# Up projection of a two-block layer: weights stationary, both halves of x as moving columns

## The chip, the cores and the metric

One core of one Trainium2 chip runs the whole program in one launch. The metric is device time in microseconds (us); lower is better.

## The reference, cut to what matters

Two layers run one after the other on x, 256 positions by 1024 features, all in float32. The change touches the MLP of the first:

```python
h2 = rms_norm(x, norm_mlp_g)
x = x + jnp.square(jax.nn.relu(h2 @ w_mlp_up)) @ w_mlp_down     # w_mlp_up 1024x4096, w_mlp_down 4096x1024
```

`rms_norm` scales each position by a positive factor r, so relu(r·a)² = r²·relu(a)², and r² may be applied after the down projection.

## The kernel before

**Products of three.** TensorE multiplies in fp32r, so each operand is split into a high part (rounded to fp32r) and a low part (the rest), and a product is high·high, high·low and low·high, summed in PSUM. Line 477 is the first, 478 multiplies by the low weights, 479 by the low activations.

**Blocks and chunks.** All weight matrices are cut into blocks of 512 columns, in program order, and each block into chunks of 4 tiles of 128 rows (`CK`). Up has 8 blocks of 2 chunks (`B_UP` to `B_UP + 7`), down 2 blocks of 8 chunks (`B_DN`, `B_DN + 1`). Four slots hold chunks. SyncE loads a chunk into `raw` (L391) once `mm_done` says that the chunk four earlier has been used; ScalarE (ACT) writes the high part `w_hi` (L1019, semaphore `split_hi`); VectorE (DVE) writes the low part `w_lo` (L1482, `split_lo`); TensorE (PE) waits for that at the first product of each chunk. `begin(b)` on ACT and DVE issues the splits of the two chunks of block b + 1 (and chunks 2 and up of block b itself, for the down blocks). Each engine does its list in order, and that order is written by hand.

**Before the change**, the activations are stationary: `mm` (L447) loads 128 columns of `s_hi` or `s_lo` and streams 512 weight columns into bank `G[b % 2][t]`, t being one of two tiles of 128 positions. That is 8 tiles x 2 x 3 = 48 products a block. DVE's `relu` (L1900) multiplies by r, takes max(0) and writes `hid`, positions on the partitions; ACT squares it (L1280); PE turns it with 8 transposes (`hidden`, L825) into the banks `M`; ACT rounds it to `hT_hi` (L1286), DVE subtracts to get `hT_lo` (L1906). Down (`mm` with `stat=(hT_hi, hT_lo)`) takes these as stationary. PE's order is block b, then the transposes of block b − 1; those of block 7 come after the first two quarters of `B_DN` (L840). `residual` (L1507) adds a down block to x. PE waits at block b for the release of block b − 2's banks (`ev0`, `ev1`). The rest of DVE's order in a middle block: two splits of the next block, relu of this one, `hidden_lo` of the last.

Of the kernel before, what the change touches and what calls it, by code (L numbers as in the profile page):

```python
# [5 lines left out]
F32 = mybir.dt.float32  # L6
# [5 lines left out]
P = 128  # L12
# [93 lines left out]
def build(nc, x_in, norm_mix_g, w_in, conv_w, a_log, dt_bias, gdn_norm_g, q_norm_g, k_norm_g, w_out,  # L106
# [4 lines left out]
    with ctx:  # L111
        def sb(name, shape, dt=F32, stack=None):
            return (stack or ctx).enter_context(nc.sbuf_tensor(name, shape, dt))
# [3 lines left out]
        def sem(name):  # L117
            if name not in named:
                named[name] = ctx.enter_context(nc.semaphore(name))
            return named[name]  # L120
# [153 lines left out]
        def st(at, n):  # L274
            return sm[:, at:at + n]
# [19 lines left out]
        SSX, RNX = st(28, 8), st(48, 16)  # L295
        XSC = st(68, 8)
        MU, VAR, RSTD = GA_, BT, EG
        RS5H, RS5Q = st(624, 2), st(626, 2)


        P2R = view(ar2, 0, NT, 2048)
# [40 lines left out]
        def at(base, step, i):  # L342
            return base if i is None else base + step * i
# [100 lines left out]
        def _(pe):  # L444
            act_w = (s_hi, s_lo)

            def mm(b, i=None, stat=act_w, turned=None, hidden=None, quarters=None):  # L447


                blk = blocks[b]  # L450
                pairs = range(blk["kt"] // 2) if quarters is None else quarters
                if b >= 2 and pairs[0] == 0:

                    pe.wait_ge(sem("ev0"), at(b - 1, 2, i))
                    pe.wait_ge(sem("ev1"), at(b - 1, 2, i))
                for pair in pairs:
                    c = 2 * pair // CK
                    n = blk["chunk0"] + c
                    kn, width = chunk_shape(b, c)
                    if b == 0:  # L460
                        pe.wait_ge(sem("split_lo" if pair % 2 else "first_lo"), c + 1)
                    elif 2 * pair == CK * c:

                        pe.wait_ge(sem("split_lo_pool" if pool_chunk(b, c) else "split_lo"), at(low_parts(b, c), 4, i))
                    if turned is not None:

                        pe.wait_ge(sem("turn_lo"), turned - KT // 2 + pair + 1)
                    if hidden is not None:

                        pe.wait_ge(sem(hidden), pair + 1)  # L470
                    early = b in EARLY and 2 * pair == blk["kt"] - 2
                    tiles = [(kt, t) for kt in (2 * pair, 2 * pair + 1) for t in range(NT)]
                    for kt, t in sorted(tiles, key=lambda tile: tile[1]) if early else tiles:
                        o = G[b % 2][t][:, 0:width]
                        hi, lo = (s[:, kt, P * t:P * t + P] for s in stat)
                        wh, wl = (s[:, n % SLOTS, kt - CK * c, 0:width] for s in (w_hi, w_lo))
                        nc.tensor.matmul(o, hi, wh, start=kt == 0, stop=False)  # L477
                        nc.tensor.matmul(o, hi, wl, start=False, stop=False)  # L478
                        last = nc.tensor.matmul(o, lo, wh, start=False, stop=kt == blk["kt"] - 1)  # L479
                        if early and t == 0 and kt == blk["kt"] - 1:  # L480
                            last.then_inc(sem("first_tile"), 1)
                    if kt == CK * c + kn - 1:
                        last.then_inc(sem("mm_done"), 1)
# [327 lines left out]

            turn(xtile, lambda q: [("ev0", B_O + 1 + q // 2), ("ev1", B_O + 1 + q // 2), ("turn_lo", 8)])

            def hidden(b, i=None):

                pe.wait_ge(sem("hid_sq"), at(b + 1, 2, i))
                for q in range(2):
                    bank = M[2 * (b % 2) + q]
                    if b >= 2 or i is not None:

                        pe.wait_ge(sem("hid_lo"), at(2 * (b - 2) + q + 1, 4, i))
                    for kk in range(2):
                        for t in range(NT):
                            c = P * (2 * q + kk)
                            last = nc.tensor.transpose(bank[:, (2 * kk + t) * P:(2 * kk + t + 1) * P], hid[:, b % 2, t, c:c + P], ident)  # L825
                    last.then_inc(sem("hid_pe"), 1)

            mm(B_UP, turned=12)
            mm(B_UP + 1)
            hidden(0)  # L830
            mm(B_UP + 2)
            hidden(1)
            with pe.Fori(0, 2) as i:
                for j in range(2):
                    mm(B_UP + 3 + j, i)
                    hidden(2 + j, i)
            mm(B_UP + 7)
            hidden(6)
            mm(B_DN, stat=(hT_hi, hT_lo), hidden="hid_lo", quarters=[0, 1])
            hidden(7)  # L840
            mm(B_DN, stat=(hT_hi, hT_lo), hidden="hid_lo", quarters=range(2, DFF // P // 2))
            mm(B_DN + 1, stat=(hT_hi, hT_lo))


            turn(xtile, lambda q: [("ev0", B_DN + 1 + q // 2), ("ev1", B_DN + 1 + q // 2), ("hid_lo", 16)])
            for j in range(4):
                mm(B_2 + j, turned=None if j else 16)

# [152 lines left out]
        def _(act):  # L1001
# [272 lines left out]
            act.wait_ge(sem("ev1"), B_UP)  # L1274
            squares(1, x)

            def square_hidden(b, i=None):
                for t in range(NT):
                    act.wait_ge(sem(f"ev{t}"), at(B_UP + b + 1, 2, i))
                    ins = nc.scalar.activation(hid[:, b % 2, t], hid[:, b % 2, t], ACT.Square)  # L1280
                ins.then_inc(sem("hid_sq"), 1)

            def hidden_hi(b, i=None):
                for q in range(2):
                    act.wait_ge(sem("hid_pe"), at(2 * b + q + 1, 4, i))
                    nc.scalar.activation(hT_hi[:, bass.ds(at(4 * b + 2 * q, 8, i), 2), :], M[2 * (b % 2) + q].rearrange("p (a b) -> p a b", a=2), ACT.Copy)\  # L1286
                        .then_inc(sem("hid_hi"), 1)

            begin(B_UP)
            square_hidden(0)  # L1290
            with act.Fori(0, 3) as i:
                for j in range(2):
                    begin(B_UP + 1 + j, i)
                    hidden_hi(j, i)
                    square_hidden(1 + j, i)
            begin(B_UP + 7)
            hidden_hi(6)
            square_hidden(7)
            hidden_hi(7)
            begin(B_DN)  # L1300
            begin(B_DN + 1)
# [159 lines left out]
        def _(dve):  # L1461
# [30 lines left out]
            def mm_finished(b, i=None):  # L1492
                dve.wait_ge(sem("mm_done"), at(blocks[b]["chunk0"] + blocks[b]["chunks"], 4, i))
# [397 lines left out]
            mean_squares(1)  # L1891
            dve.wait_ge(sem("root"), root("mlp"))

            def relu(b, i=None):
                mm_finished(B_UP + b, i)
                for t in range(NT):
                    if i is not None or b >= 2:

                        dve.wait_ge(sem("hid_pe"), at(2 * (b - 2) + 2, 4, i))
                    V.tensor_scalar(hid[:, b % 2, t], G[(B_UP + b) % 2][t][:, :], RS[:, 2 + t:3 + t], 0.0, ALU.mult, ALU.max).then_inc(sem(f"ev{t}"), 1)  # L1900

            def hidden_lo(b, i=None):
                for q in range(2):
                    dve.wait_ge(sem("hid_hi"), at(2 * b + q + 1, 4, i))
                    kk = bass.ds(at(4 * b + 2 * q, 8, i), 2)
                    V.tensor_tensor(hT_lo[:, kk, :], M[2 * (b % 2) + q].rearrange("p (a b) -> p a b", a=2), hT_hi[:, kk, :].bitcast(F32), ALU.subtract)\  # L1906
                        .then_inc(sem("hid_lo"), 1)

            begin(B_UP)
            relu(0)  # L1910
            begin(B_UP + 1)
            relu(1)
            hidden_lo(0)
            begin(B_UP + 2)
            relu(2)
            hidden_lo(1)
            with dve.Fori(0, 2) as i:
                for j in range(2):
                    begin(B_UP + 3 + j, i)
                    relu(3 + j, i)  # L1920
                    hidden_lo(2 + j, i)
            begin(B_UP + 7)
            relu(7)
            hidden_lo(6)
            hidden_lo(7)
# [365 lines left out]
```

## Time and profile before

| | us |
|---|---|
| median of 3 runs (950.75, 950.84, 953.18) | 950.84 |
| the profiled execution's own time | 952.35 |
| its span in the profile | 950.5 |
| PE busy in the span | 921.4 |
| mean granted TensorE clock | 0.993 |

Spans and starts are microseconds from the span's start. The up blocks run from about 323 to 416 us, the down blocks from there to 507 us. A matmul's row gives its start and a modelled duration that overlaps the next one's, so the pace is read from start to start.

### The profile page before, as it was taken

The page shows a single profiled execution, that of the slowest core. Times are in us where ns is not written, and L with a number is a line of the kernel's source. Part 1 is how long each engine was busy: PE and PEld are TensorE (multiplying, and loading weights), DVE is VectorE, ACT ScalarE, POOL GpSimd, SP SyncE. Part 2 cuts the span into 40 slices and gives each one's busy share as a digit, 9 for nine tenths or more (in the row PEclk, how much of TensorE's full clock was granted, in tenths as well). Part 3 has the DMA queues.
Part 4 walks back from the last instruction along what each step waited for, and adds up shares of the span by engine and source line. Part 5 has one row for each costly group of instructions (what it writes and reads, how often), then busy time and mean ns, then how long its engine had stood idle before and what let it go on. Part 6 is the DMA issues. An engine that isn't in the chain of part 4 may idle for free.

```text
span 950.5 us, 11857 instructions
## 1 busy us (share of the span) xinstructions
PE 921.4 (97%) x4691; PEld 771.8 (81%) x4691; DVE 591.9 (62%) x816; ACT 451.3 (47%) x654; POOL 124.7 (13%) x82
## 2 busy tenths in 40 slices
PE   8999999998998999999999999999998999999998
PEld 5887788876996888888887889888887888888886
DVE  4469978979456656654445745877774655555542
ACT  5265355963344544453335434753553455454531
POOL 0322112676601000000000002100000000000100
PEclk9999999999998999999999999999999999999999
DMA  7774542432312555555567645343541556554561
GB/s 268 191 247 137 177 133 89 143 124 70 95 45 85 164 193 178 177 177 177 179 192 276 208 143 174 138 133 120 181 144 44 165 164 196 183 177 133 200 221 67
DMA packets 83138, 149.87 MB, mean 158 GB/s; under 512 B 8320, under 2 KB 16048, under 8 KB 82960
## 3 DMA queue, kind: packets, MB, share of 16 engines
q1 hardware_dynamic: 79424, 144.52, 46.9%
q10 hardware_dynamic: 3040, 3.79, 1.1%
q0 software_dynamic: 624, 0.87, 0.8%
q8 instruction: 35, 0.57, 0.2%
q14 instruction: 15, 0.12, 0.0%
HBM read 147.72 MB, written 1.44 MB: 157 GB/s over the span
## 4 chain that ended last, share of the span: by engine, by line
PE 84%; DVE 7%; ACT 4%; DMA 3%; issue 1%; POOL 0%; SPq 0%; DVEq 0%; ACTq 0%
PE gemm L477 23%; PE gemm L479 23%; PE gemm L478 23%; PE mixbank L720 2%; DMA raw<-in_w_in_dram 2%; PE mixbank L612 2%; PE mixbank L587 2%; DVE w_lo L1482 1%; PE mixbank L493 1%; ACT w_hi L1019 1%; ACT junk L1175 1%; PE mixbank L825 1%; PE mixbank L598 1%; DVE mix L1599 1%; ACT mix L1187 1%
## 5 line engine op out<-in xcount | busy, mean ns | idle before, releaser
L1482 DVE TENSOR_TENSOR w_lo<-raw,w_hi 128x2048 fp32r<-128x2048 f32 (+3 forms) x131 | 287.6, 2209 | 177.5 <-ACT w_hi L1019 177.4
L477 PE MATMUL gemm<-w_hi,s_hi 128*128 128x512 f32 (+3 forms) x912 | 354.6, 389 | 11.8 <-DVE w_lo L1482 7.6
L479 PE MATMUL gemm<-w_hi,s_lo 128*128 128x512 f32 (+3 forms) x912 | 347.3, 381 | 0.0
L478 PE MATMUL gemm<-w_lo,s_hi 128*128 128x512 f32 (+3 forms) x912 | 347.1, 381 | 0.0
L1019 ACT ACTIVATE w_hi<-raw 128x2048 fp32r<-128x2048 f32 (+3 forms) x140 | 255.4, 1836 | 167.7 <-DMA raw<-in_w_in_dram 47.6
L477 PEld LDWEIGHTS gemm<-w_hi,s_hi 128*128 128x128 f32 x912 | 172.4, 189 | 46.5 <-issue 10.6
L479 PEld LDWEIGHTS gemm<-w_hi,s_lo 128*128 128x128 f32 x912 | 172.3, 189 | 32.9
L478 PEld LDWEIGHTS gemm<-w_lo,s_hi 128*128 128x128 f32 x912 | 172.6, 189 | 31.0 <-issue 0.5
L2165 POOL TENSOR_TENSOR sm<-sm 128x2 f32<-128x2 f32 (+4 forms) x14 | 29.1, 2077 | 514.4 <-DVE sm L1526 318.8
L2159 POOL TENSOR_TENSOR w_lo<-raw,w_hi 128x2048 fp32r<-128x2048 f32 x9 | 41.4, 4616 | 202.4 <-ACT w_hi L1019 202.4
L477 PE MATMUL gemm<-w_hi,hT_hi 128*128 128x512 f32 x128 | 50.6, 396 | 0.0
L478 PE MATMUL gemm<-w_lo,hT_hi 128*128 128x512 f32 x128 | 50.5, 394 | 0.0
L479 PE MATMUL gemm<-w_hi,hT_lo 128*128 128x512 f32 x128 | 50.4, 394 | 0.0
L1036 ACT ACTIVATE mix<-gemm,sm 128x512 f32<-128x512 f32 (+2 forms) x25 | 16.3, 652 | 67.8 <-PE gemm L479 67.8
L477 PE MATMUL gemm<-w_hi,h_hi 128*128 128x512 f32 x88 | 35.0, 397 | 0.2 <-DVE w_lo L1482 0.2
L479 PE MATMUL gemm<-w_hi,h_lo 128*128 128x512 f32 x88 | 34.8, 395 | 0.0
L478 PE MATMUL gemm<-w_lo,h_hi 128*128 128x512 f32 x88 | 34.8, 395 | 0.0
L1735 DVE SCALAR_TENSOR_TENSOR mix<-mixbank,cw,mix 128x255 f32<-128x255 f32 (+2 forms) x72 | 31.4, 477 | 5.4 <-ACT mix L1187 4.5
L1046 ACT ACTIVATE s_hi<-mixbank,gains 128x256 fp32r<-128x256 f32 x48 | 18.5, 488 | 21.6 <-PE mixbank L493 21.6
L477 PEld LDWEIGHTS gemm<-w_hi,hT_hi 128*128 128x128 f32 x128 | 24.0, 187 | 5.9
L479 PEld LDWEIGHTS gemm<-w_hi,hT_lo 128*128 128x128 f32 x128 | 23.9, 187 | 5.9
L478 PEld LDWEIGHTS gemm<-w_lo,hT_hi 128*128 128x128 f32 x128 | 24.0, 187 | 5.8
(300 smaller groups left out, 950.8 us busy)
## 6 DMA issues: line engine op xcount, KB each, us to landing
raw<-in_w_in_dram SPq DMA_DIRECT2D x40, 1024.0 KB, 5.1
raw<-in_w_mlp_up_dram SPq DMA_DIRECT2D x16, 1024.0 KB, 5.6
raw<-in_w_mlp_down_dram SPq DMA_DIRECT2D x16, 1024.0 KB, 5.1
raw<-in_w_gate_dram SPq DMA_DIRECT2D x10, 1024.0 KB, 5.1
raw<-in_w_up_dram SPq DMA_DIRECT2D x10, 1024.0 KB, 5.2
raw<-in_w_down_dram SPq DMA_DIRECT2D x10, 1024.0 KB, 5.2
raw<-in_w_out_dram SPq DMA_DIRECT2D x8, 1024.0 KB, 5.1
raw<-in_w_xkv_dram SPq DMA_DIRECT2D x8, 1024.0 KB, 5.2
```

What stands on the lines that cost most here:

```text
L477: nc.tensor.matmul(o, hi, wh, start=kt == 0, stop=False)
L478: nc.tensor.matmul(o, hi, wl, start=False, stop=False)
L479: last = nc.tensor.matmul(o, lo, wh, start=False, stop=kt == blk["kt"] - 1)
L587: last = nc.tensor.matmul(M[g % 2][:, j * ns:(j + 1) * ns], qq[:, P * t:P * t + P], kk[:, 0:ns], start=e == 0, stop=e == len(parts) - 1)
L612: last = nc.tensor.matmul(M[3][:, j * width:(j + 1) * width], exps_turned[:, g % 2, (j * per + s) * P:][:, 0:P], values(h, s), start=s == ...
L720: last = nc.tensor.matmul(o, lhsT[:, 4 * u + q, :], blocks_of(rhs[:, 4 * u + q, :], lv, odd), start=True, stop=True)
L1019: nc.scalar.activation(w_hi[:, n % SLOTS, 0:kn, 0:width], raw[:, n % SLOTS, 0:kn, 0:width], ACT.Copy)\
L1046: ins = nc.scalar.activation(s_hi[:, 2 * q + kk, :], M[q][:, SEQ * kk:SEQ * kk + SEQ], ACT.Copy, scale=gains[:, norm, 2 * q + kk:2 * q + k ...
L1482: V.tensor_tensor(w_lo[:, s, 0:kn, 0:width], raw[:, s, 0:kn, 0:width], w_hi[:, s, 0:kn, 0:width].bitcast(F32), ALU.subtract)\
L1735: ins = V.scalar_tensor_tensor(y, M[e % 3][:, SEQ * j:SEQ * j + SEQ - tap], cw[:, 3 - tap, ct:ct + 1], y, ALU.mult, ALU.add)
L2159: pool.tensor_tensor(w_lo[:, s, 0:kn, 0:width], raw[:, s, 0:kn, 0:width], w_hi[:, s, 0:kn, 0:width].bitcast(F32), ALU.subtract)\
L2165: pool.tensor_tensor(dst, src, MHALF[:, 0:n], ALU.pow).then_inc(sem("root"), 1)
```

## The change

The eight up blocks get their own function `up` with the weights stationary; `hid` holds turned values (features on the partitions), so the transposes go; the factor r leaves the up blocks, and the down residual multiplies by r².

```diff
-        s_hi = sb("s_hi", [P, KT, SEQ], F32R)
-        s_lo = sb("s_lo", [P, KT, SEQ], F32R)
+        s_both = sb("s_both", [P, KT, 2, SEQ], F32R)
+        s_hi, s_lo = s_both[:, :, 0, :], s_both[:, :, 1, :]
+        UP_BANKS = [[G[0][0], G[0][1], G[1][0], G[1][1]], M]
-        hid = sb("hid", [P, 2, NT, NCOL], F32, a2)
+        hid = sb("hid", [P, 8, SEQ], F32, a2)
...
 # TensorE: hidden() and the mm() calls of the up blocks go; instead
+            def up(b, i=None):
...
+                def tile_products(kt, f):
+                    n = blocks[B_UP + b]["chunk0"] + kt // CK
+                    o = UP_BANKS[b % 2][f]
+                    wh, wl = (w[:, n % SLOTS, kt % CK, P * f:P * f + P] for w in (w_hi, w_lo))
+                    nc.tensor.matmul(o[:, :], wh, s_both[:, kt].rearrange("p a b -> p (a b)"), start=kt == 0, stop=False)
+                    return nc.tensor.matmul(o[:, 0:SEQ], wl, s_hi[:, kt, :], start=False, stop=kt == KT - 1)
+                pe.wait_ge(sem("split_lo"), at(low_parts(B_UP + b, 0), 4, i))
+                for kt in range(CK):
...
+                    for f in range(4):
+                        last = tile_products(kt, f)
+                last.then_inc(sem("mm_done"), 1)
+                pe.wait_ge(sem("split_lo"), at(low_parts(B_UP + b, 1), 4, i))
...
+                for f in range(4):
+                    for kt in range(CK, KT):
+                        last = tile_products(kt, f)
+                    if f < 3:
+                        last.then_inc(sem("up_pe"), 1)
+                last.then_inc(sem("mm_done"), 1)
...
+            mm(B_DN, stat=(hT_hi, hT_lo), hidden="hid_lo")
 # ScalarE: square_hidden() goes
             def hidden_hi(b, i=None):
+                for f in range(4):
+                    act.wait_ge(sem("hid_sq"), at(4 * b + f + 1, 8, i))
+                    nc.scalar.activation(hT_hi[:, bass.ds(at(4 * b + f, 8, i), 1), :], hid[:, 4 * (b % 2) + f:4 * (b % 2) + f + 1, :], ACT.Copy)\
...
             begin(B_UP)
+            hidden_hi(0)
             with act.Fori(0, 3) as i:
                 for j in range(2):
                     begin(B_UP + 1 + j, i)
+                    hidden_hi(1 + j, i)
             begin(B_UP + 7)
             hidden_hi(7)
 # VectorE: relu() and hidden_lo() go
+            def hidden_low(b, f, i=None):
+                dve.wait_ge(sem("hid_hi"), at(4 * b + f + 1, 8, i))
...
+                V.tensor_tensor(hT_lo[:, kt, :], hid[:, n:n + 1, :], hT_hi[:, kt, :].bitcast(F32), ALU.subtract).then_inc(sem("hid_lo"), 1)
+            def relu_squares(b, i=None):
+                for f in range(4):
+                    if f < 3:
+                        dve.wait_ge(sem("up_pe"), at(3 * b + f + 1, 6, i))
+                    else:
+                        mm_finished(B_UP + b, i)
+                    o, h = UP_BANKS[b % 2][f], hid[:, 4 * (b % 2) + f, :]
+                    V.tensor_copy(h, o[:, SEQ:2 * SEQ]).then_inc(sem("up_half"), 1)
+                    dve.wait_ge(sem("up_half"), at(4 * b + f + 1, 8, i))
+                    ins = V.tensor_tensor(h, o[:, 0:SEQ], h, ALU.add)
...  # ins signals up_sum or ev0/ev1, and DVE waits for that signal
+                    V.scalar_tensor_tensor(h, h, 0.0, h, ALU.max, ALU.mult).then_inc(sem("hid_sq"), 1)
+                    if f >= 1:
+                        hidden_low(b, f - 1, i)
             begin(B_UP)
+            relu_squares(0)
+            hidden_low(0, 3)
...  # a loop over blocks 1 to 7: begin(b), relu_squares(b), hidden_low(b, 3)
+            V.tensor_tensor(RS1Q, RS[:, 2:4], RS[:, 2:4], ALU.mult).then_inc(sem("rs1"), 1)
...  # the down residual
-                residual(B_DN + j, j)
+                    V.scalar_tensor_tensor(cols, G[(B_DN + j) % 2][t][:, :], RS1Q[:, t:t + 1], cols, ALU.mult, ALU.add).then_inc(sem(f"ev{t}"), 1)
```

## Rows read from the trace of the kernel before

**Rows 1.** The page: busy time per engine, granted clock in 40 slices, chain by engine.
```profile
PE 921.4 (97%) x4691; PEld 771.8 (81%) x4691; DVE 591.9 (62%) x816; ACT 451.3 (47%) x654; POOL 124.7 (13%) x82
...
PEclk9999999999998999999999999999999999999999
...
PE 84%; DVE 7%; ACT 4%; DMA 3%; issue 1%; POOL 0%; SPq 0%; DVEq 0%; ACTq 0%
```

**Rows 2.** Busy time of one middle up block; columns: window, length, then each engine's busy time.
```profile
380.50:392.28 11.78, 11.78 (x58) 9.83 (x57) 7.19 (x6) 5.85 (x6) 0.00 (x0) 1.00 0.55 178
```

**Rows 3.** Waits between 318 and 430 us; columns: total, times, longest.
```profile
DVE w_lo L1482 <- ACT w_hi L1019: 26.0, 17, 3.4
```

**Rows 4.** Timeline of PE, up blocks; columns: start, duration, instruction, [idle before].
```profile
380.34 1.03 PE L825 MATMUL mixbank<-cst,hid 128*128 128x128 f32 x8
...
393.23 0.39 PE L478 MATMUL gemm<-w_lo,s_hi 128*128 128x512 f32 x1
...
403.68 0.39 PE L479 MATMUL gemm<-w_hi,s_lo 128*128 128x512 f32 x1
```

**Rows 5.** Timeline of PE, a block of 256 columns: first and last of 48 products.
```profile
871.62 0.28 PE L477 MATMUL gemm<-w_hi,s_hi 128*128 128x256 f32 x1
...
877.25 0.28 PE L479 MATMUL gemm<-w_hi,s_lo 128*128 128x256 f32 x1
```

**Rows 6.** Timeline of PE in the down blocks.
```profile
422.17 1.03 PE L825 MATMUL mixbank<-cst,hid 128*128 128x128 f32 x8
...
505.18 0.39 PE L478 MATMUL gemm<-w_lo,hT_hi 128*128 128x512 f32 x1
...
506.81 0.39 PE L479 MATMUL gemm<-w_hi,hT_lo 128*128 128x512 f32 x1
```

**Rows 7.** Timeline of DVE from the first up block to the last.
```profile
328.38 4.49 DVE L1482 TENSOR_TENSOR w_lo<-raw,w_hi 128x2048 fp32r<-128x2048 f32 x2 [1.71 <-ACT w_hi L1019]
334.29 1.41 DVE L1900 TENSOR_SCALAR hid<-gemm,sm 128x512 f32<-128x512 f32 x2 [1.42 <-PE gemm L479]
...
361.45 2.29 DVE L1482 TENSOR_TENSOR w_lo<-raw,w_hi 128x2048 fp32r<-128x2048 f32 x1 [1.89 <-ACT w_hi L1019]
...
415.89 1.41 DVE L1900 TENSOR_SCALAR hid<-gemm,sm 128x512 f32<-128x512 f32 x2 [2.50 <-PE gemm L479]
```

**Rows 8.** Timeline of ACT in the same stretch.
```profile
351.00 1.92 ACT L1019 ACTIVATE w_hi<-raw 128x2048 fp32r<-128x2048 f32 x1 [1.37 <-DMA raw<-in_w_mlp_up_dram]
...
359.51 1.91 ACT L1019 ACTIVATE w_hi<-raw 128x2048 fp32r<-128x2048 f32 x1
...
381.07 1.09 ACT L1286 ACTIVATE hT_hi<-mixbank 128x512 f32 x2 [4.71 <-PE mixbank L825]
...
422.80 1.09 ACT L1286 ACTIVATE hT_hi<-mixbank 128x512 fp32r<-128x512 f32 x2 [4.35 <-PE mixbank L825]
```

**Rows 9.** Groups by line and shape, DVE: total busy, mean ns | idle before.
```profile
L1745 DVE COPY mix<-mixbank 128x512 f32<-128x512 f32 x4 | 2.7, 684 | 4.3 <-PE mixbank L668 4.3
L1801 DVE COPY mix<-mix 128x256 f32<-128x256 f32 x1 | 0.4, 380 | 0.0
L2115 DVE TENSOR_TENSOR hid<-sg,gemm 128x256 f32<-128x256 f32 x2 | 0.8, 418 | 0.1
```

**Rows 10.** Groups by line and shape, ACT.
```profile
L1391 ACT ACTIVATE junk<-mix 128x256 bf16<-128x256 f32 x8 | 3.2, 404 | 2.4 <-DVE mix L1497 2.2
```

**Rows 11.** Timeline of DVE: L2051 waits for L2050's result, L1507 waits for neither.
```profile
673.22 2.28 DVE L2050 TENSOR_REDUCE sm<-mix 128x8 f32<-128x2048 f32 x1
675.53 0.17 DVE L2051 TENSOR_SCALAR sm<-sm 128x8 f32<-128x8 f32 x1
675.61 1.28 DVE L1507 TENSOR_TENSOR x<-gemm,x 128x512 f32<-128x512 f32 x2
```

**Rows 12.** Groups on DVE: with a factor per partition, and the residual without.
```profile
L1497 DVE TENSOR_SCALAR mix<-gemm,sm 128x512 f32<-128x512 f32 x21 | 15.6, 745 | 8.3 <-PE gemm L479 8.3
L1507 DVE TENSOR_TENSOR x<-gemm,x 128x512 f32<-128x512 f32 x20 | 13.3, 687 | 20.1 <-PE gemm L479 20.1
```

More of the change, by code:

```diff
@@ L297, in build @@
         MU, VAR, RSTD = GA_, BT, EG
-        RS5H, RS5Q = st(624, 2), st(626, 2)
+        RS5H, RS5Q, RS1Q = st(624, 2), st(626, 2), st(628, 2)
         P2R = view(ar2, 0, NT, 2048)
@@ L468, in mm @@
                     if hidden is not None:
-                        pe.wait_ge(sem(hidden), pair + 1)
+                        pe.wait_ge(sem(hidden), (2 if hidden == "hid_lo" else 1) * (pair + 1))
                     early = b in EARLY and 2 * pair == blk["kt"] - 2
@@ L812, in _ @@
             turn(xtile, lambda q: [("ev0", B_O + 1 + q // 2), ("ev1", B_O + 1 + q // 2), ("turn_lo", 8)])
[L814 to L833, printed above, removed]
-                for j in range(2):
[L835 to L841, printed above, removed]
+            def up(b, i=None):
+                first = b == 0 and i is None
+                if b < 2 and i is None:
+                    pe.wait_ge(sem("ev0"), B_UP)
+                    pe.wait_ge(sem("ev1"), B_UP)
+                else:
+                    pe.wait_ge(sem("ev0"), at(B_UP + b - 1, 2, i))
+                    pe.wait_ge(sem("ev1"), at(B_UP + b - 1, 2, i))
+                if b == 1 and i is None:
+                    pe.wait_ge(sem("turn_lo"), 12)
+                def tile_products(kt, f):
[6 more added lines that the diff above has]
+                for kt in range(CK):
+                    if first and kt % 2 == 0:
+                        pe.wait_ge(sem("turn_lo"), 12 - KT // 2 + kt // 2 + 1)
+                    for f in range(4):
+                        last = tile_products(kt, f)
+                last.then_inc(sem("mm_done"), 1)
+                pe.wait_ge(sem("split_lo"), at(low_parts(B_UP + b, 1), 4, i))
+                if first:
+                    pe.wait_ge(sem("turn_lo"), 12)
+                for f in range(4):
[4 more added lines that the diff above has]
+                last.then_inc(sem("mm_done"), 1)
@@ L842, in _ @@
+            up(0)
+            up(1)
+            with pe.Fori(0, 3) as i:
+                for j in range(2):
+                    up(2 + j, i)
+            mm(B_DN, stat=(hT_hi, hT_lo), hidden="hid_lo")
             mm(B_DN + 1, stat=(hT_hi, hT_lo))
-            turn(xtile, lambda q: [("ev0", B_DN + 1 + q // 2), ("ev1", B_DN + 1 + q // 2), ("hid_lo", 16)])
+            turn(xtile, lambda q: [("ev0", B_DN + 1 + q // 2), ("ev1", B_DN + 1 + q // 2), ("hid_lo", 32)])
             for j in range(4):
@@ L1293, in _ @@
                     begin(B_UP + 1 + j, i)
-                    hidden_hi(j, i)
-                    square_hidden(1 + j, i)
+                    hidden_hi(1 + j, i)
             begin(B_UP + 7)
-            hidden_hi(6)
-            square_hidden(7)
             hidden_hi(7)
@@ L1892, in _ @@
             dve.wait_ge(sem("root"), root("mlp"))
[L1894 to L1907, printed above, removed]
@@ L1909, in _ @@
-            begin(B_UP)
[L1910 to L1917, printed above, removed]
+            def hidden_low(b, f, i=None):
+                dve.wait_ge(sem("hid_hi"), at(4 * b + f + 1, 8, i))
+                kt = bass.ds(at(4 * b + f, 8, i), 1)
+                n = 4 * (b % 2) + f
+                V.tensor_tensor(hT_lo[:, kt, :], hid[:, n:n + 1, :], hT_hi[:, kt, :].bitcast(F32), ALU.subtract).then_inc(sem("hid_lo"), 1)
@@ new lines, in relu_squares @@
+            def relu_squares(b, i=None):
+                for f in range(4):
+                    if f < 3:
+                        dve.wait_ge(sem("up_pe"), at(3 * b + f + 1, 6, i))
+                    else:
+                        mm_finished(B_UP + b, i)
[3 more added lines that the diff above has]
+                    ins = V.tensor_tensor(h, o[:, 0:SEQ], h, ALU.add)
+                    if f % 2 == 0:
+                        ins.then_inc(sem("up_sum"), 1)
+                        dve.wait_ge(sem("up_sum"), at(2 * b + f // 2 + 1, 4, i))
+                    else:
+                        ins.then_inc(sem(f"ev{f // 2}"), 1)
+                        dve.wait_ge(sem(f"ev{f // 2}"), at(B_UP + b + 1, 2, i))
+                    V.scalar_tensor_tensor(h, h, 0.0, h, ALU.max, ALU.mult).then_inc(sem("hid_sq"), 1)
+                    if f >= 1:
+                        hidden_low(b, f - 1, i)
@@ L1918, in _ @@
+            begin(B_UP)
+            relu_squares(0)
+            hidden_low(0, 3)
+            with dve.Fori(0, 3) as i:
                 for j in range(2):
-                    begin(B_UP + 3 + j, i)
-                    relu(3 + j, i)
-                    hidden_lo(2 + j, i)
+                    begin(B_UP + 1 + j, i)
+                    relu_squares(1 + j, i)
+                    hidden_low(1 + j, 3, i)
             begin(B_UP + 7)
-            relu(7)
-            hidden_lo(6)
-            hidden_lo(7)
+            relu_squares(7)
@@ L1926, in _ @@
+            hidden_low(7, 3)
+            V.tensor_tensor(RS1Q, RS[:, 2:4], RS[:, 2:4], ALU.mult).then_inc(sem("rs1"), 1)
+            dve.wait_ge(sem("rs1"), 1)
             for j in range(2):
                 begin(B_DN + j)
-                residual(B_DN + j, j)
+                for t in range(NT):
+                    if j == 1 and t == 0:
+                        dve.wait_ge(sem("first_tile"), EARLY.index(B_DN + 1) + 1)
+                    else:
+                        mm_finished(B_DN + j)
+                    cols = x[:, t, NCOL * j:NCOL * j + NCOL]
+                    V.scalar_tensor_tensor(cols, G[(B_DN + j) % 2][t][:, :], RS1Q[:, t:t + 1], cols, ALU.mult, ALU.add).then_inc(sem(f"ev{t}"), 1)
```

9 lines of the change are left out of this document (removed).

## The prediction, made before the changed kernel was run

> **What bounds the kernel now.** I read the page first: PE is busy 97% of the span and 84% of the chain that ended last is PE's, at full clock [rows 1]. Then the stretch that is changed. A middle up block takes 11.78 us, all of it PE's, while DVE works 7.19 and ACT 5.85 [rows 2]. Seven such rounds lie between the first relu at 334.29 and the last at 415.89 [rows 7], 81.6 us together (the first of them, block 1, has no transposes and takes 10.9). Here PE sets the pace, and DVE has about 4.6 us to spare, most of which it waits for ACT's high parts [rows 3]. So two questions decide: what does PE's block cost afterwards, and does DVE still fit beside it?
>
> **PE's block.** 512 columns step every (403.68 − 393.23) / 46 = 0.227 us [rows 4], 256 columns every (877.25 − 871.62) / 47 = 0.120 us [rows 5]; in both streams each product has its own weight load. Before: 48 x 0.227 = 10.9, and 8 transposes, 0.79 us between them and the next product and 0.09 lost at the switch, 0.88 in all; together the 11.78 above. After: 8 tiles x 4 groups x (0.227 + 0.120) = 32 x 0.347 = 11.1 us, no transposes. The columns streamed are the same, 24,576. PE's gain is 0.67 us a block, and where nobody is late it is 81.6 − 7 x 11.1 = 3.9 us up to the end of block 7, less 0.2 for block 0 (11.1 against 10.9, without transposes), plus twice 0.88 for the transposes of blocks 6 and 7 that stand in and before the down block [rows 6]: about 5.4 us. The new step of 512 is not shown with weights stationary. The down blocks step at 1.63 / 7 = 0.233 [rows 6], the only other value of a 512 column product with this kind of operands; by it a block is 11.5. I take 0.227, since weights and x then come from the same tiles as now.
>
> **A rule on the loads.** In the 256 stream a load is issued with every product of 0.120 us, so loads lie behind products [rows 5]. The Trainium skill (TensorE: Matmul & The Clock Gate, Packing small matmuls) says that a weight load overlaps running matmuls only when it goes to another row group. By that rule the 16 loads that a block gains would stand on PE's path; the trace doesn't agree, since loads to the same rows fit within 0.120. The price of it is under the rivals.
>
> **DVE's round.** Removed per block: relu 1.41 for two [rows 7], and two subtractions of 512 columns. Added: 4 x (copy, add, max-and-square, subtract), each 256 columns. The trace has 0.418 for an op of two tensors with 256 [rows 9]; a copy of 256 within SBUF takes 0.380, but from PSUM a copy of 512 takes 0.684, as other ops do [rows 9], so I take 0.42 for all sixteen, bounds 0.38 and 0.45. An op that waits for the one before starts 0.03 after its end (673.22 + 2.28 to 675.53), one that does not starts 0.08 before it [rows 11]. Copy and add are each followed by such a wait, so 0.45 each; square and subtract step at 0.34. Quarter one takes 0.45 + 0.45 + 0.34 = 1.24, two and three 1.58 with the subtraction of the quarter before, the fourth up to the end of its square 0.45 + 0.45 + 0.42 = 1.32. Sum 5.72 us.
>
> Behind that square (time T) hangs a chain that is new. ACT now writes the high part of the last quarter after T, and only then begins the split of the next block. T + 0.03; 0.10 because the address comes from a loop register (in the loop ACT starts 381.07 − 380.34 = 0.73 after the transposes, outside it 422.80 − 422.17 = 0.63 [rows 4, 6, 8]); 0.40 for 256 columns [rows 10] less 0.1 overlap; 1.92 for the chunk's high part [rows 8]; 0.03; 2.29 for its low part [rows 7]: the first chunk is ready at **T + 4.67**, the second at T + 6.88, and DVE turns to the next quarters at T + 6.80. The round is 6.80 + 5.72 = **12.52 us**, more than PE's 11.1 and more than today's 11.78. Today this coupling is hidden: DVE waits 1.89 for the same high part [rows 7], but has slack.
>
> **From rounds to a time.** Block 0 ends at 334.29 + 0.2 = 334.5. DVE comes out of its two splits at 328.38 + 4.49 = 332.9 [rows 7], so T0 = 338.5. From there T grows by 12.52: T1 351.0, T2 363.6, T3 376.1, T6 413.6, T7 426.1. The arrival of the second chunk is not the limit: ACT starts it 5.8 after the block's end (351.00 [rows 8], where block 1 ended at 334.29 + 10.9 = 345.2), so DVE would have it by about 10.1 after the end, earlier than T + 6.88. Block b + 2 needs its first chunk at T(b) + 4.67. Block 4 would start at 334.5 + 3 x 11.1 = 367.8 and gets it at 368.2; block 5 waits 1.4, and so on 1.4 each, until the first down block starts at T6 + 4.67 = 418.3, where today it starts at 416.7 (415.89 + 0.8). Its third chunk is split behind T7, ready at 430.8, and wanted at 418.3 + 48 x 0.233 = 429.5: a further wait of 1.3. Later chunks come faster than PE takes 24 x 0.233 = 5.6 for each. Sum: +1.6 +1.3 − 0.88 (transposes of block 7) = **+2.0 us**.
>
> **Small parts.** The down residual takes 0.745 instead of 0.687 [rows 12]; the last of them stands before the next transposes: +0.06. The r² op and its wait, about 0.2, lie under DVE's wait for ACT's third chunk; without that cover +0.2. ACT drops two squares and has 4 x 0.4 instead of the two copies; it is busy under 6 us of 12.5. No DMA changes; loads follow `mm_done`, which comes at the same two points of a block. `ev0`/`ev1` of block b − 2 are given before T(b − 2), so behind the chunk's wait. The down products want `hid_lo` only pair by pair, and block 7's pairs are 39 us away. In block 0 the new order waits tile pair by tile pair as before. Total +2.1 us: 952.35 + 2.1 for the profiled execution, span about 952.6. The median of the runs is 1.5 below that execution; I forecast it: 950.84 + 2.1 = **953.0**.
>
> **Bounds of that.** Sixteen ops at 0.38 to 0.45 count fifteen times in a round and so shift it by −0.6 to +0.45. At the upper end T7 is 8 x 0.45 = 3.6 later and the sum +5.7. At the lower T7 is 4.8 earlier, 421.3, the first down block starts at 413.7, its third chunk comes 1.1 late, and the sum is −3.0 + 1.1 − 0.9 = −2.8. The 0.10 of the register may be 0 (then +1.4) or as much as 0.25, DVE's whole gap where it turns to such an op (+3.1). PE's step at 0.233 instead of 0.227 changes nothing, as PE then waits less. The granted clock is in the top tenth in all but one slice [rows 1]; I count no loss of it from gaps of 1.4 us.
>
> **Rivals.**
> 1. Faster: DVE's waits for itself cost no time. The Trainium skill (VectorE: DVE Perf Modes, The DRAIN you can't avoid) holds that the next Vector op waits for the pipe to empty in any case and a semaphore costs nothing extra. As a mechanism here, priced by rows: dependent ops would step at 0.34 too, eight times 0.11 = 0.9 less, round 11.6. Then T7 = 419, the first down block starts at 412.2 without a wait, the third chunk costs 0.4: −4.9 us, 946.0. Rows 11 speak against it (+0.03 against −0.08), on one pair of ops only. Chance 0.12, with any other cause that brings the round to PE's pace; the floor is the 5.4 above, 945.4.
> 2. Slower: bookkeeping on DVE. Each quarter has four waits, three with values from loop registers and one address from one, all in DVE's own queue; if a dependent op starts 0.10 behind instead of 0.03, eight of these make the round 13.1 and the sum +2.1 + 8 x 0.56 = +6.6, 957.4. For it: the 0.10 on ACT. Against: relu's pair of ops, with register waits between them, still overlaps (1.41 for two [rows 7], where one takes 0.745 [rows 12]). It decides from a round of 12.6 on. Chance 0.13.
> 3. Slower: a load does hang on PE. If a 512 column product cannot have its load under a 256 column one, the pair costs 0.227 + 0.19 and a block 13.3: about +12, 963. Rows 5 speak against it. Chance 0.05.
> 4. Slower: the new places of `s_hi` and `s_lo` (interleaved) bring every product that reads them to the down blocks' 0.233; 2,000 of them outside up x 0.006 = +12. No row tells what sets the 0.233. Chance 0.05.
> 5. The change does nothing (DVE's and ACT's rounds hide, and transposes were free) has no place: transposes stand on the chain. I give no chance to it apart from the sum coming out at zero, which is in the main case.
>
> **How the numbers follow.** Main case 0.65, from −2.8 to +5.7. About 0.3% (2.85 us) is what a measurement of this kernel can tell from no change. Of the 0.65, 0.44 lies within it, 0.15 above, and 0.06 is set below it, for a round at its lower end together with an error of 0.1 us in PE's block. With rival 1: faster 0.18; with rivals 2 to 4 slower 0.38. The range 946.0 to 958.0 takes in the main case and rivals 1 and 2, and leaves out 3, 4 and the floor of 1, at most 0.15. The main case's own range is 948.0 to 956.6.
>
> **What the profile after should show.** PE steps alternating 0.227 and 0.120; no L825; sixteen DVE ops a block of about 0.42; PE waits for `w_lo` of about 1.4 us at the start of blocks 5 to 7 and of the first down block, and one before its third chunk; DVE waiting some 1.4 for `w_hi` once a round; rounds 12.5 us from the third on. Rounds of 11.1 with no PE waits would be rival 1, full steps of 0.4 a pair rival 3, steps of 0.233 in the later projections rival 4. If PE's waits appear from block 2 on, the start of DVE's lag was misjudged.

## Result and the profile after

| | before | after |
|---|---|---|
| median us (runs) | 951.77 (8) | 954.77 (8) |
| lowest to highest | 950.75 to 953.19 | 953.98 to 956.60 |
| profiled execution, its span | 952.35, 950.5 | 954.18, 952.3 |
| mean granted clock | 0.993 | 0.992 |

The ratio is 1.0033, with a 95% interval of 1.0022 to 1.0044: slower by 3.0 us. Forecast were 953.0 (from 946 to 958) and no difference that can be told. The runs of before are the three of the forecast and five beside the new kernel.

The page of the changed kernel, busy time and the chain by engine, answers to [rows 1]:

```profile
PE 918.3 (96%) x4755; PEld 771.2 (81%) x4755; DVE 620.4 (65%) x913; ACT 446.7 (47%) x654; POOL 124.8 (13%) x82
...
PE 72%; DVE 14%; ACT 7%; issue 4%; DMA 3%; POOL 0%; SPq 0%; DVEq 0%; ACTq 0%
```

PE does 3.1 us less and the span is 1.8 longer. DVE does 28.5 more and its share of the chain went from 7% to 14%: the end of this kernel hangs more often on DVE. The timeline of DVE (start, duration, instruction, [idle before]) shows one whole round, that of block 2; a quarter is 128 of the block's 512 features, with one copy, one addition and one square:

```profile
357.12 0.42 DVE L1916 COPY hid<-gemm 128x256 f32<-128x256 f32 x1
357.57 0.42 DVE L1918 TENSOR_TENSOR hid<-gemm,hid 128x256 f32<-128x256 f32 x1
358.03 0.43 DVE L1925 SCALAR_TENSOR_TENSOR hid<-hid 128x256 f32<-128x256 f32 x1
358.38 0.42 DVE L1916 COPY hid<-gemm 128x256 f32<-128x256 f32 x1
...
362.46 0.42 DVE L1925 SCALAR_TENSOR_TENSOR hid<-hid 128x256 f32<-128x256 f32 x1
362.81 0.42 DVE L1906 TENSOR_TENSOR hT_lo<-hid,hT_hi 128x256 f32 x1
363.58 0.43 DVE L1906 TENSOR_TENSOR hT_lo<-hid,hT_hi 128x256 f32 x1 [0.36 <-ACT hT_hi L1297]
365.31 4.49 DVE L1490 TENSOR_TENSOR w_lo<-raw,w_hi 128x2048 fp32r<-128x2048 f32 x2 [1.31 <-ACT w_hi L1036]
369.73 0.42 DVE L1916 COPY hid<-mixbank 128x256 f32<-128x256 f32 x1
```

Read it from start to start. Copy to add 0.45, add to square 0.46, square to the next copy 0.35: the dependent and the independent step of the forecast. The round is 369.73 − 357.12 = 12.61; from block 1's round, which begins at 344.56, to block 7's, at 419.98, six rounds take 75.42, or 12.57 each. The forecast was 12.52. DVE idles 1.31 in it, for the high part that ACT could not begin earlier. ACT's timeline of the same round:

```profile
361.42 0.42 ACT L1297 ACTIVATE hT_hi<-hid 128x256 f32 x1 [1.17 <-DVE hid L1925]
363.01 0.42 ACT L1297 ACTIVATE hT_hi<-hid 128x256 f32 x1 [1.17 <-DVE hid L1925]
363.36 3.73 ACT L1036 ACTIVATE w_hi<-raw 128x2048 fp32r<-128x2048 f32 x2
```

The last square ends at T = 362.46 + 0.42 = 362.88. ACT's copy starts at T + 0.13, its split at T + 0.48 and DVE's low part at T + 2.43. ACT is idle before each quarter, yet the split of the next weights stands behind the last of them in its program. And PE's timeline: two steps in the middle of a block, then the first products of blocks 5, 6, 7, of the first down block, and of its third chunk:

```profile
323.78 0.28 PE L834 MATMUL gemm<-s_both,w_lo 128*128 128x256 f32 x1
323.90 0.40 PE L833 MATMUL gemm<-s_both,w_hi 128*128 128x512 f32 x1
324.13 0.28 PE L834 MATMUL gemm<-s_both,w_lo 128*128 128x256 f32 x1
...
380.22 0.49 PE L833 MATMUL mixbank<-s_both,w_hi 128*128 128x512 f32 x1 [0.99 <-DVE w_lo L1490]
...
392.80 0.50 PE L833 MATMUL gemm<-s_both,w_hi 128*128 128x512 f32 x1 [1.22 <-DVE w_lo L1490]
...
405.36 0.50 PE L833 MATMUL mixbank<-s_both,w_hi 128*128 128x512 f32 x1 [1.00 <-DVE w_lo L1490]
...
418.12 0.47 PE L479 MATMUL gemm<-w_hi,hT_hi 128*128 128x512 f32 x1 [1.18 <-DVE w_lo L1490]
...
430.46 0.50 PE L479 MATMUL gemm<-w_hi,hT_hi 128*128 128x512 f32 x1 [0.91 <-DVE w_lo L1490]
```

Those are the five places for which the forecast named a wait of 1.3 or 1.4; block 4, which by its sum waits 0.4, does not. The first up product starts at 322.42 here and at 323.13 before, for causes ahead of the change (in the profiles of this study it lies anywhere from 321.3 to 324.9). So I compare a **stretch** that begins with that product: up to the first down product, and from there to the first product of the projection after.

| | up | down | stretch | median us |
|---|---|---|---|---|
| before | 93.36 | 93.09 | 186.45 | 951.77 |
| after | 95.70 | 93.38 | 189.08 | 954.77 |

The stretch is 2.63 longer. One round by engine, as in [rows 2], shows DVE busy for 10.71 where a block before had 7.19, and ACT for 5.29:

```profile
344.50:357.10 12.60, 12.60 (x73) 10.90 (x72) 10.71 (x19) 5.29 (x6) 0.00 (x0) 1.00 0.54 170
```

DVE and ACT are both busy for less than the round. PE is not idle in this one, since it still has a lead over DVE from the first blocks (a block of 11.3 fits 1.1 times into the round); from 379 on the lead is used up.

### The profile page after: what moved, and what is told of

It is laid out like the page before. It is cut to its first block, busy times and chain, and to the rows that moved or that the text cites. A ratio compares the mean times of both kernels' runs of the same rounds, so it can differ in the third digit from the quotient of the medians.

```text
span 952.3 us, 12165 instructions
## 1 busy us (share of the span) xinstructions
PE 918.3 (96%) x4755; PEld 771.2 (81%) x4755; DVE 620.4 (65%) x913; ACT 446.7 (47%) x654; POOL 124.8 (13%) x82
## 4 chain that ended last, share of the span: by engine, by line
PE 72%; DVE 14%; ACT 7%; issue 4%; DMA 3%; POOL 0%; SPq 0%; DVEq 0%; ACTq 0%
PE gemm L479 20%; PE gemm L481 19%; PE gemm L480 19%; DVE w_lo L1490 4%; ACT w_hi L1036 3%; PE mixbank L722 2%; DMA raw<-in_w_in_dram 2%; PE mixbank L614 2%; PE mixbank L589 2%; DVE hid L1918 1%; DVE hid L1916 1%; PE mixbank L495 1%; DVE hid L1925 1%; ACT junk L1192 1%; ACT s_both L1063 1%
## 5 line engine op out<-in xcount | busy, mean ns | idle before, releaser
L479 PE MATMUL gemm<-w_hi,s_both 128*128 128x512 f32 (+3 forms) x784 | 304.2, 388 | 11.0 <-DVE w_lo L1490 7.4
L481 PE MATMUL gemm<-w_hi,s_both 128*128 128x512 f32 (+3 forms) x784 | 297.4, 379 | 0.0
L480 PE MATMUL gemm<-w_lo,s_both 128*128 128x512 f32 (+3 forms) x784 | 297.1, 379 | 0.0
L479 PEld LDWEIGHTS gemm<-w_hi,s_both 128*128 128x128 f32 x784 | 148.4, 189 | 40.7 <-issue 9.6
L481 PEld LDWEIGHTS gemm<-w_hi,s_both 128*128 128x128 f32 x784 | 148.3, 189 | 27.8
L480 PEld LDWEIGHTS gemm<-w_lo,s_both 128*128 128x128 f32 x784 | 148.5, 189 | 26.2 <-issue 0.5
L833 PE MATMUL mixbank<-s_both,w_hi 128*128 128x512 f32 x128 | 45.4, 399 | 2.0 <-DVE w_lo L1490 2.0
L833 PE MATMUL gemm<-s_both,w_hi 128*128 128x512 f32 x128 | 45.6, 400 | 1.7 <-DVE w_lo L1490 1.2
L1297 ACT ACTIVATE hT_hi<-hid 128x256 f32 (+1 forms) x32 | 13.4, 418 | 58.1 <-DVE hid L1925 58.1
L834 PE MATMUL gemm<-s_both,w_lo 128*128 128x256 f32 x128 | 35.9, 281 | 0.0
L834 PE MATMUL mixbank<-s_both,w_lo 128*128 128x256 f32 x128 | 35.8, 280 | 0.0
```

The source lines that it names most:

```text
L833: nc.tensor.matmul(o[:, :], wh, s_both[:, kt].rearrange("p a b -> p (a b)"), start=kt == 0, stop=False)
L834: return nc.tensor.matmul(o[:, 0:SEQ], wl, s_hi[:, kt, :], start=False, stop=kt == KT - 1)
```

## Experiments

**Theories.** A, that of the forecast: PE could do the new blocks faster than the old ones, but a chain through DVE and ACT (last square, ACT's copy of the quarter, high part and then low part of the next weights) sets the pace at 12.57. B: PE's own stream got slower, by its loads. C: the new layout of x or the down residual costs something elsewhere. The runs of before that each kernel is compared with were made beside it: a median of 952.04 (20 runs) in 1, 2, 3 and the first of 4, and of 952.02 (10 runs) in the second of 4 and in 5.

### 1. The split no longer behind the last quarter

```diff
 # ScalarE, hidden_hi(b)
                 for f in range(4):
+                    if f == 2:
+                        split(B_UP + b + 2, 0, i) if b < 7 or i is not None else split(B_DN, 2)
                     act.wait_ge(sem("hid_sq"), at(4 * b + f + 1, 8, i))
...
-                    begin(B_UP + 1 + j, i)
+                    split(B_UP + 2 + j, 1, i)
                     hidden_hi(1 + j, i)
```

> The changed kernel with one move on ScalarE: the high part of the first chunk of the block after next is written between the second and third quarter of a block instead of behind its fourth. Nothing is added or left out. Theory (the round of VectorE, which waits for ScalarE's high part, sets the pace of the up blocks): VectorE's round falls from 12.57 us by its wait of 1.3 and, with it, below PE's 11.3, so PE sets the pace, its waits for w_lo before blocks 5 to 7 and in the down block (1.0 to 1.2 each) go, and the stretch from the first up product to the first product of the next projection falls from 189.1 us to 8 x 11.3 + 89.7 + 2.6 = 182.8; the kernel comes out 3.6 us under the kernel before, about 948.2. Rival (PE's own pace with the weights stationary, 0.353 a pair, is what costs): the stretch stays near 189 and the time near 954.8.

Measured: 947.42 (5 runs), ratio 0.9950, interval 0.9937 to 0.9964; stretch 88.83 + 92.13 = 180.95. That is 8.1 less than the changed kernel and 5.5 less than before, and faster than both. The waits between 318 and 435 us (total, times, longest) hold none of PE for `w_lo`; that of DVE, which was 15.4 us in 10 waits in the changed kernel, is now harmless:

```profile
DVE w_lo L1495 <- ACT w_hi L1036: 10.5, 5, 3.3
```

ACT's timeline shows where the work went, into ACT's idle time between the quarters:

```profile
359.50 0.42 ACT L1299 ACTIVATE hT_hi<-hid 128x256 f32 x1 [0.83 <-DVE hid L1930]
359.82 1.90 ACT L1036 ACTIVATE w_hi<-raw 128x2048 fp32r<-128x2048 f32 x1
361.63 0.40 ACT L1299 ACTIVATE hT_hi<-hid 128x256 f32 x1
362.67 0.42 ACT L1299 ACTIVATE hT_hi<-hid 128x256 f32 x1 [0.65 <-DVE hid L1930]
```

and DVE's goes from its last subtraction straight on:

```profile
363.24 0.43 DVE L1911 TENSOR_TENSOR hT_lo<-hid,hT_hi 128x256 f32 x1 [0.36 <-ACT hT_hi L1299]
363.66 4.49 DVE L1495 TENSOR_TENSOR w_lo<-raw,w_hi 128x2048 fp32r<-128x2048 f32 x2
```

The same 16 ops a block and the same splits are done. Only the order of ACT's program differs, and PE never waits. A holds; B falls, since eight blocks with all their loads take 88.83, or 11.10 each. The expectation had used the pair of the first profile, 0.354, where this one has 0.347; that is the subject of 6.

### 2. The halves not side by side

```diff
-                    nc.tensor.matmul(o[:, :], wh, s_both[:, kt].rearrange("p a b -> p (a b)"), start=kt == 0, stop=False)
+                    nc.tensor.matmul(o[:, 0:SEQ], wh, s_hi[:, kt, :], start=kt == 0, stop=False)
+                    nc.tensor.matmul(o[:, 0:SEQ], wh, s_lo[:, kt, :], start=False, stop=False)
...
-                    V.tensor_copy(h, o[:, SEQ:2 * SEQ]).then_inc(sem("up_half"), 1)
-                    dve.wait_ge(sem("up_half"), at(4 * b + f + 1, 8, i))
-                    ins = V.tensor_tensor(h, o[:, 0:SEQ], h, ALU.add)
+                    ins = V.tensor_scalar(h, o[:, 0:SEQ], 0.0, None, ALU.max)
```

> The changed kernel with the products of the high and the low half of x no longer side by side: three products of 256 columns each go to the same 256 columns, so PSUM adds them and VectorE's copy and addition become one maximum read from PSUM. Same result. PE streams the same columns with 96 loads a block instead of 64. Theory (VectorE's round is the bound): four times 0.45 us less, a round of 10.8, below PE's block, so PE sets the pace: 96 x 0.118 to 0.120 = 11.3 to 11.5 us a block, 3.6 to 2.0 us under the kernel before, 948.2 to 949.8. Rival 1 (PE's pace or its loads are the cost): 32 more loads a block make it no better than 954.8, and if a load hangs out of a product, 96 x 0.19 = 18 us a block and over 1000. Rival 2 (ScalarE's order alone is the cost, whatever VectorE has to do): no change from 954.8.

Measured: 949.78 (9 runs), ratio 0.9976 (0.9965 to 0.9986), stretch 92.22 + 92.13 = 184.35, up block 11.53, no wait of PE for `w_lo`. Three products of 256 in PE's timeline, every 0.120:

```profile
329.86 0.28 PE L833 MATMUL gemm<-s_both,w_hi 128*128 128x256 f32 x1
329.98 0.28 PE L834 MATMUL gemm<-s_both,w_hi 128*128 128x256 f32 x1
330.10 0.28 PE L835 MATMUL gemm<-s_both,w_lo 128*128 128x256 f32 x1
```

This is the upper end of what the theory gave, and both rivals fall: the time is not at 954.8 or above it, although ACT's order is the one of the changed kernel. A shorter round of DVE removes PE's waits just as the move in 1 does. Side by side saves PE 0.360 − 0.347 = 0.013 a tile and group (0.006 where a pair takes 0.354, see 6), and costs DVE an op of 0.45 a quarter. Where DVE sets the pace, that trade loses: with the sum left to PSUM, the turned values alone are 2.1 better than before.

### 3. The small parts alone

The kernel before, with the interleaved `s_both` and the factor at the down residual (relu keeps its op, with 1.0 for the factor):

```diff
-        s_hi = sb("s_hi", [P, KT, SEQ], F32R)
-        s_lo = sb("s_lo", [P, KT, SEQ], F32R)
+        s_both = sb("s_both", [P, KT, 2, SEQ], F32R)
+        s_hi, s_lo = s_both[:, :, 0, :], s_both[:, :, 1, :]
...
-                residual(B_DN + j, j)
+                    V.scalar_tensor_tensor(cols, G[(B_DN + j) % 2][t][:, :], RS1Q[:, t:t + 1], cols, ALU.mult, ALU.add).then_inc(sem(f"ev{t}"), 1)
```

> The kernel before with two parts of the change alone: the interleaved places of the high and low half of x, and the norm factor taken out of relu and put squared at the down residual. Theory: within 1 us of the kernel before (the last residual op is 0.06 longer). Rival (the new places slow every product that reads them from 0.227 to 0.233, or the residual costs more than that): 2 to 12 us slower.

Measured: 951.30 (11 runs), ratio 0.9989 (0.9978 to 1.0001), stretch 186.48 against 186.45. C falls: rival 4 with it, and the small parts cost nothing.

### 4. More work for PE, with and without the wait

To the changed kernel, and to that of 1, eight products of 256 columns a block, which are written over and change nothing:

```diff
+                    if kt == 0:
+                        for _ in range(2):
+                            nc.tensor.matmul(o[:, 0:SEQ], wl, s_hi[:, kt, :], start=True, stop=True)
                     nc.tensor.matmul(o[:, :], wh, s_both[:, kt].rearrange("p a b -> p (a b)"), start=kt == 0, stop=False)
```

> The changed kernel with 8 more products of 256 columns a block on PE (two ahead of the first of each quarter, overwritten by it), 8 x 0.118 = 0.94 us a block, 7.5 us in all. Theory (PE has 1.24 us to spare in a round of 12.57): the extra work goes into PE's waits for w_lo, the rounds stay at 12.57, and the time stays within 1 us of the changed kernel, about 954.8. Rival (PE sets the pace): 7.5 us more, 962.

> The changed kernel with ScalarE's split moved forward (as in e1_split_first) and the 8 more products of 256 columns a block on PE (as in e4_more_pe), 7.5 us of PE's time in all. Theory (with the move PE sets the pace from the first block to the last): all 7.5 us come through, stretch 180.95 + 7.5 = 188.5, time 947.4 + 7.5 = 954.9; without the move only 1.2 of them did. Rival (VectorE's round still bounds, only shorter): less than 4 us more, under 951.5.

Measured, in the changed kernel: 955.32 (6 runs), ratio 1.0034 (1.0022 to 1.0046), stretch 98.20 + 92.12 = 190.32. In that of 1: 955.95 (7 runs), ratio 1.0040 (1.0025 to 1.0054), stretch the same 190.32. The extra work is 64 x 0.120 = 7.7 us. It costs the changed kernel 1.2 and the other one 9.4 of the stretch, and 0.6 and 8.5 in the medians. So the changed kernel had about 6.4 us of PE's time to give away, and with more work for PE the order of ACT's program matters no longer. The 9.4 is 1.7 more than the work; see 6.

### 5. More work for DVE

One copy more a quarter, from PSUM into a tile that nobody reads:

```diff
+                    V.tensor_copy(spare[:, :], o[:, 0:SEQ])
                     V.tensor_copy(h, o[:, SEQ:2 * SEQ]).then_inc(sem("up_half"), 1)
```

> The changed kernel with one more copy of 256 columns from PSUM a quarter on VectorE, into a tile that nobody reads: 4 x 0.34 = 1.36 us a block, waits for nothing. Theory (VectorE's round is the bound and its length counts for every block): the round goes from 12.57 to 13.93, the end of the last square comes 8 x 1.36 = 10.9 us later, and the stretch goes from 189.1 to about 200, the time to about 965.5. Rival (PE's pace or the waits for ScalarE are the cost and VectorE has room): under 2 us more.

Measured: 966.42 (4 runs), ratio 1.0152 (1.0127 to 1.0176), stretch 104.93 + 94.96 = 199.88. The rounds start 13.9 apart: 4 x 0.34 = 1.36 more, one for one. PE's waits grew, and after one of 2.34 its products are slow (PE's timeline):

```profile
369.24 0.28 PE L835 MATMUL mixbank<-s_both,w_lo 128*128 128x256 f32 x1
369.35 0.40 PE L834 MATMUL mixbank<-s_both,w_hi 128*128 128x512 f32 x1
369.59 0.28 PE L835 MATMUL mixbank<-s_both,w_lo 128*128 128x256 f32 x1
372.22 0.52 PE L834 MATMUL gemm<-s_both,w_hi 128*128 128x512 f32 x1 [2.34 <-DVE w_lo L1491]
372.55 0.39 PE L835 MATMUL gemm<-s_both,w_lo 128*128 128x256 f32 x1
372.75 0.63 PE L834 MATMUL gemm<-s_both,w_hi 128*128 128x512 f32 x1
373.17 0.41 PE L835 MATMUL gemm<-s_both,w_lo 128*128 128x256 f32 x1
373.39 0.63 PE L834 MATMUL gemm<-s_both,w_hi 128*128 128x512 f32 x1
```

A pair takes 0.64 instead of 0.354 (372.75 to 373.39) until about 375.9. The busy times by round (window, length, busy time and instructions of PE, PEld, DVE, ACT and POOL, granted clock, DMA share, GB/s) show DVE busy for 12.0 of 13.9, and a granted clock under 1 in the second, which is part of it at 1.2 GHz and the rest at 2.4; the last row, inside the slow pairs, has 0.50, the lower level:

```profile
346.50:360.40 13.90, 12.77 (x72) 10.83 (x71) 12.01 (x24) 5.28 (x6) 0.00 (x0) 1.00 0.60 184
360.40:374.30 13.90, 11.56 (x61) 9.81 (x60) 11.96 (x24) 5.32 (x6) 0.00 (x0) 0.94 0.57 185
372.60:375.60 3.00, 3.00 (x11) 2.61 (x10) 2.93 (x5) 0.00 (x0) 0.00 (x0) 0.50 0.67 257
```

As PE is the one that waits here, its slow pairs cost no time in a round: the wait behind the slow block comes out shorter (1.22, against 2.63 before it, from start to start of the products).

### 6. Whose is the step of a pair?

In the first profile of the changed kernel a product of 512 columns steps at about 0.236 and one of 256 at 0.118 in blocks 0 to 4, a pair of 0.354; the profile in 1 has 0.230 and 0.117, a pair of 0.347; both profiles in 4 have 0.354. The changed kernel once more, unchanged:

> The changed kernel once more, unchanged, for a second profile. In the first its pair of products stepped at 0.236 + 0.118 = 0.354 us, in e1_split_first, whose PE instructions are the same, at 0.230 + 0.117 = 0.347. If the step belongs to the execution, it may differ here; if to the kernel, it is 0.354 again. Rounds of 12.57 and a stretch of 189.1 in either case, since PE waits for the difference.

Measured: 953.44 (1 run), and the rounds and the stretch as in the first (189.02). Now blocks 0 to 3 have a pair of 0.347, so PE is earlier and one more wait appears, at block 4. PE's timeline, first and last product of blocks 4, 5 and 6:

```profile
366.51 0.50 PE L833 MATMUL gemm<-s_both,w_hi 128*128 128x512 f32 x1 [0.60 <-DVE w_lo L1490]
...
377.81 0.28 PE L834 MATMUL gemm<-s_both,w_lo 128*128 128x256 f32 x1
379.07 0.49 PE L833 MATMUL mixbank<-s_both,w_hi 128*128 128x512 f32 x1 [0.98 <-DVE w_lo L1490]
...
390.15 0.28 PE L834 MATMUL mixbank<-s_both,w_lo 128*128 128x256 f32 x1
391.64 0.50 PE L833 MATMUL gemm<-s_both,w_hi 128*128 128x512 f32 x1 [1.21 <-DVE w_lo L1490]
...
402.93 0.28 PE L834 MATMUL gemm<-s_both,w_lo 128*128 128x256 f32 x1
```

Each block is the same 64 products, and from its first start to its last it takes 11.30, 11.08 and 11.29. So the pair changes inside one execution: 0.353 in block 4, 0.347 in block 5, 0.353 in block 6, and 0.347 again in block 7. In the first profile it is 0.354 in blocks 0 to 4 and 0.347 in block 5, then 0.353 in blocks 6 and 7. Each change stands behind a wait of PE, and not every wait brings one; between two waits the pair stays the same, also over blocks 0 to 3, which write to the two sets of banks in turn.

Then the kernel of 1 once more, and that of 4 with both edits twice more; before, run beside them, took 955.52 (1 run, mean granted clock 0.989).

> The kernel with the earlier split alone, once more. Nothing waits in its up blocks, so its stretch is 256 pairs of 512 and 256 columns and the down blocks: 180.9 with a step of 0.347 as before. If the step belongs to the execution, it may come at 0.354 this time: stretch 182.7, execution 950.0. If it is set by the instructions: 0.347, stretch 180.9, about 947.4 to 948.3.

> The kernel of the run with both the earlier split and eight more products, profiled once more, for the step of a pair (512 and 256 columns), which was 0.354 there and 0.347 with the earlier split alone. If the step is set by this kernel's instructions, it is 0.354 again, the stretch 190.3 and the execution about 957.8. If it belongs to the execution, a profile with a step near 0.347 exists: 256 pairs x 0.007 = 1.8 us less, stretch about 188.5 and the execution about 956 or below. That would also say that the times of that kernel, which lie from 954.2 to 956.0 and at 957.7 to 957.8, are of two kinds for this reason.

> A third profile of the kernel with both edits, for the same question: step 0.354 and stretch 190.3 in every profile if the instructions set it; any mixture of 0.347 and 0.354 if the execution does, with the execution's own time lower by 1.8 us where the step is 0.347.

The kernel of 1 took 950.40, with a stretch of 90.52 + 92.12 = 182.65: now its pair is 0.354, from the first up product to the last, where in its first profile it was 0.347 throughout. That is 1.7 us more in 256 pairs, with no wait of PE in either. So the instructions don't set the step; it belongs to a run of products between two waits of PE, and the kernel of 1 has one such run for all its up blocks. The kernel with both edits had 0.354 in all three profiles (stretch 190.33, 190.32, 190.33) at times of 957.83, 957.22 and 955.22: the expectation that its lower times come from the faster pair is not borne out. They come from ahead of the stretch, whose first product starts at 324.85, 324.37 and 322.12. What sets the step when PE starts again stays open.

With equal steps of 0.354 the sums close. Kernel 1 (182.65) plus 7.68 of extra work is 190.33: measured 190.32. The changed kernel (189.08) less kernel 1 (182.65) is 6.4, what its waits cost; the extra work fills them, and 7.68 − 6.43 = 1.25 is what comes through: measured 1.24.

## Why the prediction was right, and how far

**The pace, right.** The step that decided, "T + 4.67" for the first chunk behind the last square and a round of 12.52, is measured as T + 4.73 for PE's first product (block 5, which hangs on block 3's last square: T = 375.49, start 380.22) and 12.57. Experiment 1 takes the chain out of PE's way and 5 lengthens the round; both times PE's waits follow. The 0.42 an op, the dependent 0.45 and the independent 0.34 held to 0.01.

**Where the time went.** In the words of the sum: +1.6, +1.3 and −0.88. The waits before the first down block brought +2.34 (95.70 − 93.36) instead of +1.6. The third chunk's wait and the transposes of block 7 brought +0.29 (93.38 − 93.09) instead of +0.42; experiment 1, which has no such wait, shows them apart: −0.97 without it (92.12 − 93.09), +1.26 by it. The 2.0 of the forecast came out as 2.63. The term that was undersized is the first, by 0.74. T6, counted from the first up product, came 0.3 later (six rounds 0.05 longer each). The first down product started 4.92 behind T6 (413.20, 418.12) instead of 4.67, though DVE's two splits began at the forecast place (415.57; T6 + 2.38 was forecast). It starts 2.55 behind that split in both profiles of the changed kernel, an up block's first product 2.34 or 2.35, and no row tells why. And the forecast took the old start of the down block as 416.7, where it is 416.49.

**The rest of the 3.0.** The stretch grew by 2.63, the profiled execution by 1.83, the medians by 3.00. Up to 3.6 us of shift ahead of the stretch stand between single executions, so the profiled execution's 1.8 is not evidence against the 2.6. The forecast gave its largest chance, 0.44, to a difference within 0.3% (2.85 us). The measured 3.00 lies just outside, and its interval (0.22% to 0.44%) reaches to both sides, so the runs show a difference, but not on which side of that bound. The mechanism is what was right; on which side of "no difference" the time fell was luck, by 0.15 us. The time itself, 954.77 against 953.0, is off by 1.8, and 0.9 of it is the base: the forecast added to the median of three runs, 950.84, and the eight have 951.77.

**A slip in the bounds.** With ops of 0.38 us, T6 is 7 x 0.6 = 4.2 earlier and the first down block starts at 409.4 + 4.67 = 414.1, not 413.7. Its third chunk is then 0.7 late instead of 1.1, so the sum of −2.8 and the range stay.

**PE's block.** "PE's step at 0.233 instead of 0.227 changes nothing, as PE then waits less" was right: 11.3 in blocks 0 to 4 of the first profile, 11.1 by the forecast, and nothing came of it but that block 4 had no wait. In the repeated one, with 11.1 in blocks 0 to 3, it has one of 0.60.

**The rule on the loads.** PE did 64 products and 64 loads a block where it did 48, and its block went from 11.78 to 11.1 (kernel 1): a load of 128x128 hides under a product of 512 and of 256 columns, to the same rows. The rule weighed in the forecast (the Trainium skill, TensorE: Matmul & The Clock Gate, Packing small matmuls) is not what this stream does. Rival 3 falls.

**Rival 1** (DVE's waits for itself are free) falls by the rows of DVE: 0.45 behind a wait for itself, 0.35 without. The sentence cited for it (the Trainium skill, VectorE: DVE Perf Modes, The DRAIN you can't avoid) disagrees with them by 0.1 us an op. **Rival 2** (0.10 per dependent op) falls too: such an op starts 0.03 after the end of the one before. **Rival 4** falls by experiment 3. The 5.4 us that PE has to gain without waits are real: kernel 1 got 5.5 with the faster pair and 3.8 with the slower.

## What to carry to other kernels

A change that moves work from the busiest engine to one with slack is priced by the chain that the next round of work must pass, and not by the sum of busy time: here DVE had 4.6 us to spare in a block, took 3.5, and the block still grew. Look at what stands behind a new wait in the program of a third engine. ACT was busy for 5.3 us of a round of 12.6, but the next weights' split stood behind its wait for the last quarter, and moving that one split between two quarters turned 3.0 us lost into 4.6 gained.

## What was not expected of the hardware

- The step of the same matmul stream is not always the same: 0.347 or 0.354 for a pair of 512 and 256 columns. In the kernel of 1, where PE does not wait in the up blocks, it was the one in one execution and the other in another, which is 1.7 us of 950. In the changed kernel it changed between blocks of one execution, each time behind a wait of PE. The granted clock was 1.00 in the up blocks of these profiles. The down blocks' step of 512 columns was about 0.233 in each profile with a full clock there, that of the projections on either side 0.227. Nothing in the runs tells what sets it.
- In the stretch, after waits of up to 1.38 us, PE's products went on at full pace, but for 0.1 in the first. After the waits of 2.34, 2.35 and 2.70 in experiment 5 the next products ran at the lower clock of 1.2 GHz (granted 0.50): a pair took 0.64, and 512 columns 0.43 where the level of 2.4 GHz shows 0.236 at most. These stretches have no wait between 1.38 and 2.34 us. In the stretch the changed kernel has none as long and a granted clock of 1.00; its mean of 0.992 comes from before the stretch, where PE waits 4.39 us at 235 and 3.76 at 293 and the granted clock is 0.96 from 200 to 280 and 0.66 from 290 to 300.
